# Two successive rows per partition for the experts' down matrices, and features taken at a stride of four to match

## The reference, cut to what matters

```
hid = jax.nn.silu(jnp.einsum('becd,edf->becf', xg, w_gate)) * jnp.einsum('becd,edf->becf', xg, w_up)
out = jnp.einsum('becf,efd->becd', hid, w_down) * g.astype(h.dtype)[..., None]
```

## Time and profile before

| | |
|---|---|
| median of 3 runs | 2594.79 us (2594.1 to 2595.84) |
| the profiled execution | 2593.67 us |
| its span in the trace | 2591.8 us |
| TensorE busy | 2362.2 us, 91% |
| TensorE weight loads | 1811.6 us, 70% |
| VectorE busy | 1783.2 us, 69% |
| ScalarE busy | 1415.4 us, 55% |
| moved by DMA | 585.56 MB |

### The profile page before, as it was taken

One profiled execution on the slowest core, in us unless ns is written; L12 is line 12 of the kernel. 1 busy time (PEld: TensorE's weight loads), 2 busy tenths in 40 slices (PEclk: granted clock), 3 DMA queues, 4 the chain that ended last, 5 costly groups with the idle time before them and its releaser, 6 DMA issues.

```text
span 2591.8 us, 34527 instructions
## 1 busy us (share of the span) xinstructions
PE 2362.2 (91%) x13256; PEld 1811.6 (70%) x13256; DVE 1783.2 (69%) x1987; ACT 1415.4 (55%) x1440; POOL 204.1 (8%) x220
## 2 busy tenths in 40 slices
PE   6999998789849999999999968988984999999994
PEld 4887776568736666666666647876864788888883
DVE  5523212454587888888888767566658899999995
ACT  6310112664526566666656654557353777777774
POOL 0000000000010111211111010000000011111110
PEclk9999999899969999999999989999997999999997
DMA  6034546545317877887887861112345999999995
GB/s 246 25 106 133 164 146 126 220 181 203 122 55 279 290 290 280 291 302 291 291 305 280 305 198 29 29 37 77 123 177 193 352 380 398 390 388 387 388 377 182
DMA packets 194342, 585.56 MB, mean 226 GB/s; under 512 B 19657, under 2 KB 64449, under 8 KB 187713
## 3 DMA queue, kind: packets, MB, share of 16 engines
q1 hardware_dynamic: 178688, 529.61, 54.8%
q0 software_dynamic: 12336, 48.24, 7.2%
q10 hardware_dynamic: 3216, 6.29, 0.7%
HBM read 536.88 MB, written 47.21 MB: 225 GB/s over the span
## 4 chain that ended last, share of the span: by engine, by line
PE 84%; DVE 6%; ACT 5%; DMA 3%; issue 2%; SPq 0%; POOL 0%; ACTq 0%; POOLq 0%; DVEq 0%
PE ps L1588 14%; PE ps L1590 13%; PE ps L1589 13%; PE ps L1603 6%; PE ps L571 5%; PE ps L572 4%; PE ps L573 4%; PE ps L796 3%; PE ps L798 3%; PE ps L797 3%; PE ps L508 1%; PE ps L608 1%; PE ps L542 1%; PE ps L610 1%; PE ps L609 1%
## 5 line engine op out<-in xcount | busy, mean ns | idle before, releaser
L1814 DVE TENSOR_TENSOR R_H_r<-R_M,R_W_r 128x2048 fp32r<-128x2048 f32 x336 | 758.9, 2287 | 140.9 <-ACT R_W_r L1716 138.6
L1716 ACT CAST R_W_r<-R_M 128x2048 fp32r<-128x2048 f32 x336 | 640.0, 1916 | 215.6 <-PE ps L1590 214.5
L1590 PE MATMUL ps<-R_W_r,R_C_r 128*128 128x512 f32 x1536 | 605.4, 394 | 0.0
L1588 PE MATMUL ps<-R_W_r,bc_r 128*128 128x512 f32 x1024 | 411.3, 402 | 5.8 <-ACT R_W_r L1716 2.9
L1589 PE MATMUL ps<-R_H_r,bc_r 128*128 128x512 f32 x1024 | 402.9, 393 | 0.0
L1590 PEld LDWEIGHTS ps<-R_W_r,R_C_r 128*128 128x128 f32 x1536 | 288.4, 188 | 65.9
L1588 PEld LDWEIGHTS ps<-R_W_r,bc_r 128*128 128x128 f32 x1024 | 192.2, 188 | 65.4 <-issue 10.9
L571 PE MATMUL ps<-R_H_r,R_W_r 128*128 128x512 f32 (+1 forms) x632 | 232.4, 368 | 4.9 <-ACT R_W L2177 2.0
L572 PE MATMUL ps<-R_C_r,R_W_r 128*128 128x512 f32 (+1 forms) x632 | 229.0, 362 | 0.0
L573 PE MATMUL ps<-R_H_r,R_W_r 128*128 128x512 f32 (+1 forms) x632 | 228.7, 362 | 0.0
L1589 PEld LDWEIGHTS ps<-R_H_r,bc_r 128*128 128x128 f32 x1024 | 192.3, 188 | 42.5
(11 more groups left out here) (322 smaller groups left out, 3769.5 us busy)
## 6 DMA issues: line engine op xcount, KB each, us to landing
R_M<-in_moe_w_gate SPq DMA_DIRECT2D x114, 1024.0 KB, 8.4
R_M<-in_moe_w_down SPq DMA_DIRECT2D x112, 1024.0 KB, 8.1
R_M<-in_moe_w_up SPq DMA_DIRECT2D x110, 1024.0 KB, 7.4
bc<-in_ada_w SPq DMA_DIRECT2D x28, 1024.0 KB, 4.9
R_H<-in_moe_w_up SPq DMA_DIRECT2D x18, 1024.0 KB, 7.2
R_H<-in_moe_w_down SPq DMA_DIRECT2D x16, 1024.0 KB, 8.8
R_H<-in_moe_w_gate SPq DMA_DIRECT2D x14, 1024.0 KB, 7.8
R_W<-in_ev_w_in SPq DMA_DIRECT2D x25, 512.0 KB, 3.9
```

Source lines behind the costliest of these rows:

```text
L1588: pe.matmul(o, hi[:, k, :], wh[:, kk, cs], start=(k == 0), stop=False)
L1590: ins = pe.matmul(o, lo[:, k, 0:P], wh[:, kk, cs], start=False, stop=(k == KC - 1))
L1716: nc.scalar.copy(whi[j], raw[slot + j]).then_inc(unit_high_done, 1)
L1814: nc.vector.tensor_tensor(wlo[j], raw[slot + j], whi[j], ALU.subtract).then_inc(unit_low_done, 1)
```

## The change

The down matrices are loaded with other rows on each partition. Before, partition p of unit j held rows 256j + p and 256j + 128 + p. Now the matrix is cut in halves h of 512 rows, and partition p of unit j = 2h + q holds rows 512h + 4p + 2q and 512h + 4p + 2q + 1, which follow each other in memory (8 KB). A unit is still one transfer of 1 MB into the same slot. Gate and up matrices are loaded as before. The hidden features on partition p of group k must then be 512(k div 4) + 4p + (k mod 4), so each transpose reads 128 columns of `hid` that lie four apart instead of side by side. The same holds for the four transposes of the context's hidden values. Everything behind the transposes is as before.

```diff
-            w = [I[x].rearrange("l e (j k p) n -> (l e j) p k n", j=4, p=P)
-                 for x in ("moe_w_gate", "moe_w_up", "moe_w_down")]
+            w = [I[x].rearrange("l e (j k p) n -> (l e j) p k n", j=4, p=P) for x in ("moe_w_gate", "moe_w_up")]
+            w_down = I["moe_w_down"].rearrange("l e (h p q k) n -> (l e h) q p k n", h=2, q=2, p=P)
...
-                    src = w[m][(n0 + e) * 4 + j] if isinstance(e, int) else \
-                        w[m][bass.ds((n0 + e) * 4 + j, 1)].rearrange("a p k n -> p (a k) n")
+                    if m == 2:
+                        src = w_down[(n0 + e) * 2 + j // 2, j % 2] if isinstance(e, int) else \
+                            w_down[bass.ds((n0 + e) * 2 + j // 2, 1), j % 2].rearrange("a p k n -> p (a k) n")
+                    else:
+                        src = w[m][(n0 + e) * 4 + j] if isinstance(e, int) else \
+                            w[m][bass.ds((n0 + e) * 4 + j, 1)].rearrange("a p k n -> p (a k) n")
...
                 for k in range(KC):
-                    ins = pe.transpose(ps[:, 2 + k // 4, (k % 4) * P:(k % 4 + 1) * P], hid[:, k * P:(k + 1) * P],
+                    ins = pe.transpose(ps[:, 2 + k // 4, (k % 4) * P:(k % 4 + 1) * P], hid[:, 512 * (k // 4) + k % 4:512 * (k // 4 + 1):4],
                                        ident[:, :])
...
                     for k in range(4):
-                        ins = pe.transpose(ps[:, hidden_bank, k * 2 * C:(k + 1) * 2 * C], hidc[0:2 * C, k * P:(k + 1) * P],
+                        ins = pe.transpose(ps[:, hidden_bank, k * 2 * C:(k + 1) * 2 * C], hidc[0:2 * C, k:512:4],
                                            ident[0:2 * C, 0:2 * C])
```

## The result

The changed kernel took 2599.49 us (median of 20 runs, 2594.75 to 2606.82), the kernel before 2593.81 us (20 runs, 2590.40 to 2598.32). The ratio is 1.0022, with a 95% interval from 1.0016 to 1.0028. That is 5.7 us slower, at the edge of the 0.2% named in the prediction and clear of its interval. The profiled execution took 2600.0 us with a span of 2598.1, 6.3 more than before.

A forecast was written before the change was run, and what follows sets the result against it. TensorE's own sequence was taken to bound the kernel. Transfers 0, SP 0, latent transposes 12.8 and context transposes 3.2 gave +16.0 us, a time of 2611 us; own range 2608 to 2614, wider range 2592 to 2616.

The forecast's parts named there:

- two of the rivals: Transposes: a free stride, loads stay 140 ns, 2594.8 us, chance 0.28; a hidden longer load, 2599 to 2601, chance 0.12.
- The longer load: Latent transposes' weight load on TensorE: median near 190 ns instead of 140, a set of eight 1.27 us.
- the constant 0.05 us looks like the weight load, in series with the stream: TensorE's transposes: load time adds to stream time, so 320 strided loads cost 0.050 us more each, 16.0 us.
- The line through three distances: Transpose distances 0.108, 0.079, 0.066 us at 128, 64, 32 streamed columns, read as 0.05 us plus 0.46 ns per column.
- the hidden load: Rival, transposes: the next load runs under the current stream, the longer sets the distance; 2599 to 2601 us, chance 0.12.
- Its terms of 1.8 and 2.3 us: Hidden-load rival's costs for 256 latent and 64 context transposes with a load 50 ns longer, together 4.1 us.
- The packets: Down loads: 8 KB packets, so 6272 fewer of 47316 from 2060 to 2530 us.
- The cover of the loads: Second layer needs 380 GB/s, undisturbed rate 410, so a third of loads could become about 22% slower before binding.
- Faster through lighter traffic: Rival, expert matmuls: larger pieces remove collisions with arriving data, 3072 matmuls gain 3.2 ns each, 9.8 us, 2585; chance 0.05.

The follow-up runs named there:

- lighter work: Kernel before with one of three expert matmuls and nearly all of VectorE's work on expert weights left out, so that transfers bound: 2419.37 us, ratio 0.9320.
- either right kernel: The changed kernel (columns four apart), 2599.49 us, and one with both halves at a step of two and matching rows, 2599.72 us, ratio 1.0023 to the kernel before.
- Two kernels whose transfers bound: Kernel before and changed kernel, each with part of TensorE's and VectorE's work on expert weights left out: 2419.37 us and 2409.52 us.

## Why the prediction was wrong

**The direction and the place were right.** The kernel became slower, in the transposes, on TensorE's path. The transfers were worth nothing, as predicted: the loads alone gave 1.0002.

**The number.** The forecast was 2611 us and 16 us of loss; 5.7 us were measured. The time lies within the range of 2592 to 2616 only because that range takes in two of the rivals. It isn't in the forecast's own range of 2608 to 2614. The prediction had named the sign that came: it is wrong if the load is longer but the set stays near 0.9 us. The load took 209 ns and the set 0.95 us.

**The longer load.** Predicted near 190 ns, measured 209. The row of the ordinary float32 load, 192 ns, was the nearest one, but no run shows that the two have the same cause.

**The step that failed** is "the constant 0.05 us looks like the weight load, in series with the stream". By it each of 320 loads was charged its 50 ns. Measured per transpose are 10 ns for the 256 latent ones, 2.6 us and not 12.8, and 57 ns for the 64 of the context, 3.7 us and not 3.2. The load runs beside the stream of another transpose, and the longer of the two sets the distance. With 128 streamed columns the stream set 0.108 us, and a load bound that went from 0.064 to 0.120 shows only its last 0.01. With 64 the load set the distance already, and the whole 0.057 shows. The context, which has a fifth of the transposes, makes up more than half of the loss.

**The line through three distances** was what misled me. The three rows differed in partitions and in their number of transposes as well as in streamed columns. The 0.079 us at 64 columns is a mean of three distances, of which the first is 0.11, where the set begins behind transposes on 128 partitions. The other two are 0.064, and so is the distance at 32 columns (0.066 in the prediction, whose row has such a first distance too). From 64 columns down the distance doesn't change: it isn't a line but a floor. The argument against the hidden load, "0.079 at 64 streamed columns is above a floor of 0.065", came from that mean.

**The rival that held** is the hidden load, chance 0.12, 4.1 to 6.7 us for 5.7 measured (6.2 by the trace). Its mechanism, the larger of load and stream, is what the runs show. Its terms of 1.8 and 2.3 us for a load 50 ns longer were 2.6 and 3.7 in the trace. The context's was too small because it, too, started from 0.079 and not from 0.064.

**The packets.** The prediction wanted 49 x 128 = 6272 fewer from 2060 to 2530 us and left out the seven down units of that stretch that land in R_H. With all 56 of the kernel before it would have been 56 x 128 = 7168. Measured are 39,973 packets where there were 47,316, so 7343 fewer.

**The cover of the loads.** I wrote that a third of the loads could become 22% slower before they bound the second layer. The pace of 34.40 us with lighter work against 35.05 leaves about 1.9% over all of them, some 6% on a third. It did no harm here, since they became quicker.

**Faster through lighter traffic** didn't happen: with the loads alone the pace stayed at 35.04 us.

## What to carry to other kernels

Before a weight load is priced as part of a transpose, look at what streams meanwhile: the same 70 ns cost 10 ns under 128 streamed columns and 57 under 64. Read the distance in the middle of a row of instructions, since the first one can hold something else. Larger pieces for a transfer are a gain only where transfers bound, so measure the pace of the loads by themselves before paying for them elsewhere. An order that one operand must match moves its price to whichever engine makes the permutation; look for slack there first.

## What the runs showed of the hardware

At the full granted clock (1.00 in the windows of the experts) TensorE loads 128 contiguous float32 columns of a transpose in 138 to 143 ns by the medians from offsets 0 to 3, and steps of 2 to 8 take 195 to 228 ns. Two columns apart is as dear as four: 209 ns in either right kernel. The Trainium skill, Advanced Engine Details and Errata, section SBUF Cachelines, asks for at least two accesses to a line of 16 bytes. A step of two has them and still takes 195 to 209 ns, so here the measurement decides against that as the threshold. Within a set, strided transposes follow one another at 0.120 us with 128, 64 or 32 streamed columns, contiguous ones at 0.108, 0.064 and 0.064. Why a load recorded with 209 ns sets a distance of 0.120 us stays open. So does the reason for the jump at a step of two.

VectorE's product of 128 by 1024 went from 1214 to 2035 ns when neighbouring values were written 512 bytes apart, in groups of four. Two kernels whose transfers bound moved 396 and 399 GB/s in the second layer (windows 1950 to 2350 us) with pieces of 4 KB and with a third of 8 KB.
